# Norms whose sums GpSimd gathers whole, with TensorE's sum and broadcast placed later

## The reference

```python
def rmsnorm(x, w):
    y = xf * lax.rsqrt(jnp.mean(xf * xf, axis=-1, keepdims=True) + EPS)
    return (y * w).astype(x.dtype)
def modulate(x, w, shift, scale):
    return rmsnorm(x, w) * (1 + scale) + shift
for l in range(DEPTH):      # ctx likewise, through the same weights
    x = x + 0.5 * g1 * swiglu(modulate(x, nw[0], sh1, sc1), ffn1_up[l], ffn1_down[l])
    x = x + g2 * token_mixer(modulate(x, nw[1], sh2, sc2), ...)
    x = x + 0.5 * g3 * swiglu(modulate(x, nw[2], sh3, sc3), ffn2_up[l], ffn2_down[l])
return rmsnorm(x, final_norm_w)
```

## Time and profile before

| | |
|---|---|
| median of 3 runs | 3034.98 us (3033.96 to 3035.81) |
| the profiled execution | 3036.34 us, of it the span 3034.6 us |
| TensorE busy | 2969.7 us (98%) |
| VectorE, ScalarE, GpSimd busy | 1621.1, 810.8, 213.3 us |
| mean granted TensorE clock | 0.991 |

### The profile page before, as it was taken

The page is one execution under the profiler, slowest core; times in us unless marked ns, Lnnn a source line. Parts: engine busy times, 40 slices in busy tenths (PEclk is TensorE's granted clock), DMA queues, the critical chain, the costliest instruction groups (busy, mean ns, idle before and its releaser), DMA issues.

```text
span 3034.6 us, 41426 instructions
## 1 busy us (share of the span) xinstructions
PE 2969.7 (98%) x16228; PEld 2539.7 (84%) x16228; DVE 1621.1 (53%) x2706; ACT 810.8 (27%) x1094; POOL 213.3 (7%) x212
## 2 busy tenths in 40 slices
PE   7999999999999999999999999999999899999998
PEld 5888888888888888888888888888888688888886
DVE  6676776557433348776765762222246744533333
ACT  3211211243232232212112421121234333332223
POOL 1000000102600010000000100000010500100001
PEclk8999999999999999999999999999999999999999
DMA  6444434222112224444442432212113123333331
GB/s 214 121 115 132 118 111 139 71 57 49 25 49 62 69 65 137 132 118 132 118 132 70 118 91 63 63 55 70 51 42 84 36 61 95 97 90 97 97 95 64
DMA packets 455616, 273.62 MB, mean 90 GB/s; under 512 B 9754, under 2 KB 453828, under 8 KB 455492
## 3 DMA queue, kind: packets, MB, share of 16 engines
q1 hardware_dynamic: 453348, 267.90, 31.0%
q10 hardware_dynamic: 2144, 4.00, 0.4%
HBM read 269.77 MB, written 2.10 MB: 90 GB/s over the span
## 4 chain that ended last, share of the span: by engine, by line
PE 90%; DVE 6%; ACT 2%; issue 1%; DMA 0%; SPq 0%; DVEq 0%; ACTq 0%
PE ps L1251 54%; PE ps L1258 27%; PE ps L1418 2%; PE ps L1282 1%; PE ps L1423 1%; DVE hlo L1805 1%; DVE htmp L1795 1%; DVE states L1063 1%; PE ps L703 1%; PE ps L672 1%; DVE first_acc L1749 1%; PE ps L683 1%; PE ps L1300 1%; ACT whi L1512 0%; DMA first_mod<-in_w_mod 0%
## 5 line engine op out<-in xcount | busy, mean ns | idle before, releaser
L1251 PE MATMUL ps<-hhi,whi 128*128 128x512 f32 x3136 | 892.0, 352 | 1.2 <-ACT whi L1512 1.2
L1251 PE MATMUL ps<-hlo,whi 128*128 128x512 f32 x3136 | 881.0, 348 | 0.0
L1682 DVE TENSOR_TENSOR wlo<-wraw,whi 128x1024 fp32r<-128x1024 f32 x371 | 456.9, 1232 | 591.6 <-ACT whi L1512 588.6
L1512 ACT ACTIVATE whi<-wraw 128x1024 fp32r<-128x1024 f32 x371 | 391.3, 1056 | 934.0 <-PE ps L1258 912.8
L1258 PE MATMUL ps<-hhi,wlo 128*128 128x512 f32 x3136 | 630.8, 350 | 0.0
L1251 PEld LDWEIGHTS ps<-hhi,whi 128*128 128x128 f32 x3136 | 501.9, 188 | 83.8 <-issue 3.1
L1258 PEld LDWEIGHTS ps<-hhi,wlo 128*128 128x128 f32 x3136 | 502.1, 188 | 81.3 <-issue 1.0
L1251 PEld LDWEIGHTS ps<-hlo,whi 128*128 128x128 f32 x3136 | 501.2, 188 | 80.3 <-issue 0.5
L1696 DVE SCALAR_TENSOR_TENSOR macc<-modraw,cond,macc 128x256 f32<-128x256 f32 x896 | 365.4, 479 | 0.1
L1251 PE MATMUL ps<-mhi,whi 128*128 128x512 f32 (+1 forms) x1184 | 334.3, 349 | 4.1 <-DVE mlo L1949 2.9
L1251 PE MATMUL ps<-mlo,whi 128*128 128x512 f32 (+1 forms) x1184 | 332.7, 348 | 0.0
(11 more groups left out here) (189 smaller groups left out, 2342.0 us busy)
## 6 DMA issues: line engine op xcount, KB each, us to landing
wraw<-in_ffn_up SPq DMA_DIRECT2D x176, 512.0 KB, 3.9
modraw<-in_w_mod SPq DMA_DIRECT2D x66, 1024.0 KB, 5.2
wraw<-in_ffn_down SPq DMA_DIRECT2D x64, 512.0 KB, 3.8
wraw<-in_w_in SPq DMA_DIRECT2D x64, 512.0 KB, 4.0
wraw<-in_ffn_down SPq DMA_DIRECT2D x32, 384.0 KB, 3.2
wraw<-in_w_out SPq DMA_DIRECT2D x16, 512.0 KB, 3.7
first_mod<-in_w_mod SPq DMA_DIRECT2D x6, 1024.0 KB, 12.1
wraw<-in_w_br_pool SPq DMA_DIRECT2D x16, 256.0 KB, 2.8
```

The source lines that it names most:

```text
L1251: nc.tensor.matmul(o, whi[:, slot, k, :], a[:, k * NT + t0:k * NT + t0 + n], start=(k == 0 and a is hi), stop=False)
L1512: nc.scalar.activation(whi[:, slot2], wraw[:, slot4], ACT.Copy).then_inc(hi_split, 1)
L1682: nc.vector.tensor_tensor(wlo[:, slot2], wraw[:, slot4], whi[:, slot2].bitcast(F32), ALU.subtract).then_inc(lo_split, 1)
```

## The change

All eight squares of a half are added by GpSimd, so `ssq` is complete and TensorE sums one set per half (4 or 2 matmuls in place of 12 or 6). The first half's sum moves behind the second context product, its broadcast behind the third. The second half's sum moves from ahead of chunk 2 of `first_pair` to ahead of chunk 4, its broadcast from ahead of chunk 4 to ahead of chunk 6 (in the fifth tail it stays ahead of chunk 7).

```diff
             norm, split = norm + 1 + two, split + two
-            sq_count, used_count = sq_count + (DC + DC // 2 if two else DC), used_count + (DC if two else SQ_ADDED)
+            sq_count, used_count = sq_count + (DC + DC // 2 if two else DC), used_count + (DC + DC // 2 if two else SQ_ADDED)
...
             def norm_sum_ahead(ph, half):
-                norm_sum((ph["ahead"][half],), ph["used"] + SQ_ADDED + 2 * half, ph["sq"] + DC + half * DC // 2)
+                blocks_in = part_blocks(ph["ahead"][half])
+                pe.wait_ge(sq_used, ph["used"] + DC + half * DC // 2)
+                for b in blocks_in:
+                    mm = nc.tensor.matmul(bank(7, 256 + b, 1), ssq[:, b * P:(b + 1) * P], ones[:, 0:1],
+                                          start=True, stop=True)
+                mm.then_inc(var_ready, 1)
...
                     if n_ph and before["ahead"]:
-                        if (n_pt, k) == (0, 2):
+                        if (n_pt, k) == (0, 4):
                             norm_sum_ahead(before, 1)
-                        if (n_pt, k) == (0, 4 if before["ahead"] is BOTH else DC - 1):
+                        if (n_pt, k) == (0, 6 if before["ahead"] is BOTH else DC - 1):
...
                 products_ahead(ph, 0, ph["ahead"][1], kk)
+                products_ahead(ph, 1, ph["ahead"][1], kk)
                 norm_sum_ahead(ph, 0)
-                products_ahead(ph, 1, ph["ahead"][1], kk)
+                products_ahead(ph, 2, ph["ahead"][1], kk)
                 norm_spread(ph["norm"], ph["ahead"][:1], jobs_before(ph))
-                products_ahead(ph, 2, ph["ahead"][1], kk)
                 products_ahead(ph, 3, ph["ahead"][1], kk)
...
-                act.wait_ge(sq_used, ph["used"] + (j - 1 if s < 2 or half == 0 else j + 1))
+                act.wait_ge(sq_used, ph["used"] + (j - 1 if s < 2 or half == 0 else j + 3))
...
                     for half in range(2 if ph["ahead"] else 0):
-                        for s in range(2):
-                            add_squares(DC // 2 + s, (ph["ahead"][half],), ph["sq"] + DC // 2 * (1 + half) + s + 1,
-                                        ph["used"] + DC // 2 + 2 * half + s + 1)
+                        for s in range(DC // 2):
+                            n = DC // 2 * (1 + half) + s + 1
+                            add_squares(DC // 2 + s, (ph["ahead"][half],), ph["sq"] + n, ph["used"] + n)
```

## The result

The changed kernel takes 3048.41 us (median of 5 runs, 3047.4 to 3050.71) against 3034.98 (5 runs beside them, 3031.66 to 3035.81): ratio 1.0046, 95% interval 1.0036 to 1.0057. It is 13.4 us slower; 3048.9 was forecast.

A forecast was written before the change was run, and what follows sets the result against it. TensorE, busy 98% of the span, was taken as the bound, but VectorE's htmp of chunk 8 as setting each tail's end. Tails 7.5, GpSimd 1.5 and clock 4.9 sum to 13.9 us slower: median 3048.9, range 3041.5 to 3053.

The forecast's parts named there:

- The second sum, the step that decides: Ahead of chunk 4 in first_pair: hhi of chunk 4 queues behind ScalarE's second root, so TensorE idles 1.7 us.
- B: Date of a tail's first htmp on VectorE, after the first half's broadcast.
- First half: Context products, sum and broadcast up to the first htmp: 8.00 us, 10.1 with 24 matmuls; GpSimd's adds cost nothing.
- U to B: Time from a tail's first context product to its first htmp: forecast 8.00 us, 10.1 with 24 matmuls a product.
- From B to the end: From the first htmp to the end of first_pair: forecast 26.24 us, set by chunk 8's htmp.
- B to C: Time from a tail's first htmp to chunk 8's htmp: forecast 16.07 us.
- C to E: Time from chunk 8's htmp to the end of the tail's first_pair: forecast 10.17 us, as before.
- The tails: Later ends of the five first_pairs: +1.0, +2.8, +0.2, +1.7 and an estimated +1.8, sum 7.5 us.
- GpSimd beside VectorE: Second half's adds for chunks 6 and 7 overlap hlo of chunks 2 and 3: 0.3 us per tail, 1.5 in all.
- The clock: Idle around chunk 4 lowers TensorE's clock: 1.3 us per fall, three-in-four chance in each of five tails, 4.9 us.
- the relay is mostly hidden: Rival: later phases absorb one or two microseconds per tail, so the change comes out even, 3035 to 3041 us; chance 0.13.
- TensorE is the limit all through: Rival: if chunk 4's hhi needs no root ahead, 112 fewer rows and spared falls give about 3020 us; chance 0.06.

The follow-up runs named there:

- Experiment 2: Changed kernel with ScalarE's second root behind hhi of chunk 5 and VectorE's reciprocal behind hlo of chunk 5; TensorE's places kept: 3036.12 us, ratio 1.0004.
- experiment 3: Changed kernel with the first half's sum and broadcast at their places of before, the second half as changed: 3046.39 us, ratio 1.0038.
- experiment 4: Changed kernel with both sums and both broadcasts at their places of before, leaving only GpSimd's added squares: 3032.39 us, ratio 0.9991.
- experiment 5: Kernel before with only the sums and broadcasts moved as in the change, TensorE still summing three sets: 3066.9 us, ratio 1.0105.
- experiment 1: Changed kernel with the second half's sum back ahead of chunk 2 and its broadcast ahead of chunk 4: 3037.14 us, ratio 1.0009.
- experiment 6: Changed kernel with the second root late, behind chunk 5, and the first half's sum and broadcast at their places of before: 3029.89 us, ratio 0.9982.
- experiment 7: Changed kernel with the second root late and the first half's broadcast right behind its sum, ahead of the third context product: 3026.82 us, ratio 0.9978.

## Why the prediction was right

*The second sum, the step that decides: right.* TensorE was to start the sum at B + 10.66 and chunk 4 at B + 12.89; it did at B + 10.69 and B + 12.94 (632.06 and 634.31 less 621.37). The idle was to be 1.7 and was 1.75. Experiment 2 shows the cause by taking only ScalarE's and VectorE's order away: 12.3 us come back.

*First half: right.* U to B was to be 8.00, and 10.1 in tail 2; it was 7.91 to 7.92, and 10.05. Of the falls of before the prediction read those in tails 1 and 4 and not the two in tail 3, but since it subtracts whole tails they are in its differences all the same. GpSimd was ahead of the sum, as worked out; experiments 3 and 4 show it 0.75 late where the sum stands one product sooner.

*From B to the end: right, a little short.* TensorE was to wait some 0.9 ahead of chunks 2 and 3 and for chunk 1 too; it waited 0.59 ahead of each of the two and not for chunk 1, and nothing came of it, since VectorE sets the dates there. B to C was to be 16.07 and was 16.30 to 16.32 where the clock held. From C to E it was to be 10.17 and was 10.16 to 10.18.

*The tails.* Forecast +1.0, +2.8, +0.2, +1.7 and, as an estimate, +1.8: 7.5. Measured, less about 1.5 for tail 3's fall of the clock and 1.6 for tail 5's (3.77 - 2.2): +1.15, +2.99, +0.37, +1.88, +1.6: 8.0, in which tail 5's 1.6 holds the 0.34 of GpSimd that comes next. Even so the differences of tails 1 to 4 were 0.7 above the forecast: B to C was 0.23 longer than worked out and U to B 0.08 shorter, in four tails. Some 0.2 of the 0.23 lie in chunks 4 and 5, which take 637.26 - 634.31 = 2.95 and not 2.75, in part since the first matmul after the idle holds the next one up (634.31 to 634.65, 0.34, where the following ones are 0.23 apart).

*GpSimd beside VectorE: mis-sized, 0.3 and not 1.5.* GpSimd's timeline of tail 1 has the add for chunk 6, and VectorE's `hlo` at 627.51, shown above, begins within it:

```profile
626.94 0.74 POOL L2010 TENSOR_TENSOR ssq<-ssq,sq 128x256 f32<-128x256 f32 x1 [6.00 <-ACT sq L1544]
```

The add ends at 627.68, 0.17 into `hlo`, as the walk said; but `hlo` takes 0.75, as it does alone. In tail 5 the overlap is longer, and there `hlo` is held up:

```profile
2652.14 0.72 POOL L2010 TENSOR_TENSOR ssq<-ssq,sq 128x256 f32<-128x256 f32 x1 [5.16 <-ACT sq L1544]
2652.50 0.65 DVE L1812 SCALAR_TENSOR_TENSOR hlo<-htmp,modv,hhi 128x256 fp32r<-128x256 f32 x1 [0.49 <-ACT hhi L1589]
```

It takes 0.65 where an `hlo` of that width takes 0.48, with an overlap of 0.36, and chunk 3's does the same; in the kernel before and in experiment 5, which have no add at that place, the same two passes take 0.48 to 0.49. TensorE waits for both, so this is 0.34 us, all of it in tail 5. The Trainium skill, SBUF — State Buffer, "Who interferes with whom", would have the two exclude each other. The subtraction in the earlier trace rows and tail 5's `hlo` agree with that; the last 0.17 us of the add in tail 1 don't show it.

*The clock: mis-sized, about 3.1 and not 4.9.* Two of five tails fell, not three to four, and each cost 1.5 to 1.6, not 1.3. Of how many fall, one profiled execution is no measure: experiments 1, 3 and 5 have falls in tails in which the change has none. Experiments 2, 6 and 7, which have no idle at chunk 4, have none in any tail; but the kernel before and experiments 1 and 4 have no idle at chunk 4 either, and have falls in two, three and one of their pairs (experiments 1 and 4 with an idle of up to 2.24 ahead of chunk 2, before with one of 0.66). So what brings them about stays open. Nor is the term what the clock did to the change as a whole: the tails of before spent 13.7 us at 0.50 and those of the change 6.8.

GpSimd is 1.2 less than forecast, the clock 1.8 less and the stall 0.2 more (8.0 less the 0.34, against 7.5), so 11.1 in place of 13.9; with the 1.28 ahead of tail 1, which is scatter of the start, and the rest of -0.3 that is the profiled +12.07. The median came out 0.5 under the forecast since before's profiled run lay 1.36 above its median and after's lay on it: that the median was met so closely is partly luck, since two terms that were too high were made up by the scatter and by the offset of before's profile; that its distance is a stall of 8 us with some falls of the clock is not.

*The rivals.* That the relay is mostly hidden is refuted by the tails: 11.1 of 12.07 us are in them and nothing behind gave any back. That TensorE is the limit all through is refuted at the point that was named for it: `hhi` of chunk 4 does stand behind the root. Experiment 2 meets its condition by changing that order, yet came to 3036, not the 3020 of that rival. With the order mended VectorE still sets the end of a tail, with a B to C of 14.33 where before had 13.99 to 14.41, and TensorE goes on waiting ahead of chunks 0, 2 and 3 (1.25, 0.57 and 0.59 in tail 1). So busy time taken off TensorE between B and C is worth little. What is worth something is an earlier B that doesn't lengthen B to C by as much: experiment 7 has it 1.4 earlier than the change in tail 1, gives 0.34 of it back against experiment 2, and comes to 3026.8.

## What to carry to other kernels

Moving a sum later on the engine that computes it moves every engine's answer to it: look at what stands behind the root in ScalarE's written order, and whether the first engine has work left to cover the relay sum, root, next chunk, `hlo` (here 1.75 us in four tails and 1.27 in the fifth, and 12.3 us in all with what follows from them). When a synchronising step goes later on one engine, move its partner on the others by as much, behind the work that doesn't need it; or ask first whether it has to move at all, since here the tails came out level with the second sum left in place (experiment 4) and moved with its partner (experiment 6). A saving of busy time on the bound engine (here 12.1 us) is worth what its waits leave of it: 2.8 us at the old places, 7.8 with the best places and order found.

## What the runs showed of the hardware that I had not expected

- Idle of 1.75 us ahead of chunk 4 left the granted clock at 1.00 in tails 1, 2 and 4 and brought it to 0.50 in tail 3, with the same instructions and, against tails 1 and 4, to 0.02 us the same gaps. What makes the difference isn't in these rows, and stays open. The Trainium skill, TensorE: Matmul & The Clock Gate, "What's actually happening", says that the throttle is the default and that activity releases it; the prediction read it so that every tail would fall, and three of five did not.
- What such a fall costs depends on where it lies: 1.5 us in B to C where TensorE's products are on the way to chunk 8's `htmp` (17.80 against 16.30 to 16.32), and 0.7 to 0.8 where B to C stays as it is (C to E of 10.86 and 11.01 in experiment 1, 11.01 in experiment 4, against 10.18). The runs of one kernel spread with the clock: in experiment 1 the fastest, 3033.0, has a mean of 0.993 and the slowest, 3044.93, one of 0.988.
- GpSimd's adds for a half come 2.24 us too late for a sum at chunk 2 of a pair that follows on the change's first half (experiment 1, tails 1 to 4), and 0.75 us too late for one behind the first context product of a tail with 18 matmuls in a product (experiments 3, 4 and 6); with 24 matmuls they are in time.
- A VectorE `hlo` of 256 columns takes 0.65 us in place of 0.48 when a GpSimd add of 256 columns still runs for the first 0.36 of it, and one of 512 columns takes 0.75, as alone, when the add ends 0.17 into it.
